# Moving a sample's past scores to just behind a job's values, in the differential-attention rounds of a decoder step

## The reference, cut to what matters

```
p = probs(q1, k1) - lam * probs(q2, k2)     # softmax each, over all keys
o = einsum('bhts,bshd->bthd', p, v)
# prompt: keys = its own 512 tokens, causal
# sample: keys = 1024 past keys from the pages, then its 8 new ones
```

## Time and profile before

| what | value |
|---|---|
| median of 3 runs | 2305.47 us (2305.38 to 2305.98) |
| the profiled execution, its own time | 2303.8 us |
| its span, first to last instruction | 2302.0 us |
| mean granted clock of TensorE | 0.979 of full |
| differential rounds (first past scores to last values) | 127.0 to 274.3 us of the span |
| first past scores to the last sample's past scores, 7 rounds | 127.0 to 257.6 us, 18.7 us a round |

### The profile page before, as it was taken

How to read it: one execution, slowest core, us unless ns; L and a number is a source line. 1 busy time by engine, 2 the same in 40 slices (tenths; PEclk the granted TensorE clock), 3 DMA queues, 4 the chain that set the end, 5 groups by cost and what they waited for, 6 DMA issues and landing times.

```text
span 2302.0 us, 37427 instructions
## 1 busy us (share of the span) xinstructions
PE 2121.5 (92%) x15226; PEld 1875.4 (81%) x15230; DVE 1233.9 (54%) x2035; ACT 708.7 (31%) x1085; POOL 269.8 (12%) x243
## 2 busy tenths in 40 slices
PE   8978899989998999999999899888998999999997
PEld 6745688778877999999997577567987999999996
DVE  4346456755543566426544799564433466524642
ACT  5233344432231322212233425342322322212222
POOL 0012101530100100000002235320100100000001
PEclk9999999989999999999999999999999999999998
DMA  5366423323343222222224124642343222222221
GB/s 184 112 213 221 156 65 105 125 78 129 119 176 115 81 74 83 74 83 78 74 80 119 49 81 160 202 129 73 122 155 133 82 74 78 79 83 74 83 70 58
DMA packets 220861, 249.28 MB, mean 108 GB/s; under 512 B 18498, under 2 KB 175436, under 8 KB 220486
## 3 DMA queue, kind: packets, MB, share of 16 engines
q1 hardware_dynamic: 199162, 196.22, 26.9%
q0 software_dynamic: 9936, 28.78, 3.9%
q10 hardware_dynamic: 11592, 21.88, 2.8%
HBM read 233.63 MB, written 13.00 MB: 107 GB/s over the span
## 4 chain that ended last, share of the span: by engine, by line
PE 76%; DVE 12%; issue 5%; ACT 3%; DMA 2%; PEld 2%; POOL 1%; PEldq 0%; DVEq 0%; POOLq 0%; SPq 0%; ACTq 0%
PE PS L831 52%; PE PS L810 5%; PE PS L888 5%; PE PS L1244 1%; DVE arena L3189 1%; PE PS L1259 1%; DVE arena L3187 1%; DVE arena L3222 1%; DVE arena L3219 1%; DVE stat L2516 1%; PE PS L1431 1%; DVE arena L2423 1%; PE PS L1560 1%; PE PS L964 1%; PEld PS L1097 1%
## 5 line engine op out<-in xcount | busy, mean ns | idle before, releaser
L831 PE MATMUL PS<-hT_r,WH 128*128 128x288 f32 (+2 forms) x1856 | 554.0, 298 | 21.7 <-issue 17.1
L831 PE MATMUL PS<-xr_r,WH 128*128 128x288 f32 (+2 forms) x1920 | 571.6, 298 | 1.6 <-POOL W_r L658 1.6
L831 PE MATMUL PS<-hT_r,W_r 128*128 128x288 f32 (+2 forms) x1856 | 549.7, 296 | 0.0
L2380 DVE TENSOR_TENSOR W_r<-W,WH 128x1024 fp32r<-128x1024 f32 (+1 forms) x219 | 284.0, 1317 | 375.1 <-ACT WH L1695 374.3
L831 PE MATMUL PS<-arena_r,WH 128*128 128x224 f32 (+2 forms) x1920 | 441.5, 298 | 3.7 <-issue 3.7
L1695 ACT ACTIVATE WH<-W 128x1024 fp32r<-128x1024 f32 (+1 forms) x262 | 266.1, 1034 | 501.3 <-PE PS L831 275.8
L831 PEld LDWEIGHTS PS<-hT_r,WH 128*128 128x128 f32 x1856 | 350.2, 189 | 35.0 <-issue 31.6
L831 PEld LDWEIGHTS PS<-xr_r,WH 128*128 128x128 f32 x1920 | 364.0, 190 | 2.3 <-issue 2.3
L831 PEld LDWEIGHTS PS<-hT_r,W_r 128*128 128x128 f32 x1856 | 350.3, 189 | 0.0
L831 PEld LDWEIGHTS PS<-arena_r,WH 128*128 128x128 f32 x1920 | 326.9, 190 | 6.4 <-issue 6.3
L831 PE MATMUL PS<-arena_r,W_r 128*128 128x288 f32 (+2 forms) x704 | 208.6, 296 | 0.0
(11 more groups left out here) (439 smaller groups left out, 3054.6 us busy)
## 6 DMA issues: line engine op xcount, KB each, us to landing
W<-in_w_ffn_in SPq DMA_DIRECT2D x176, 256.0 KB, 3.3
W<-in_w_ffn_out SPq DMA_DIRECT2D x40, 512.0 KB, 3.4
W<-in_w_in_ab SPq DMA_DIRECT2D x28, 512.0 KB, 3.7
C<-in_cache_mem_k SPq DMA_DIRECT2D x10, 1024.0 KB, 7.8
C<-in_cache_diff_k POOLq DMA_DIRECT2D x32, 256.0 KB, 4.0
C<-in_cache_diff_k SPq DMA_DIRECT2D x32, 256.0 KB, 3.3
C<-in_cache_diff_v POOLq DMA_DIRECT2D x32, 256.0 KB, 5.1
C<-in_cache_diff_v SPq DMA_DIRECT2D x32, 256.0 KB, 4.9
```

The costliest lines, as they stand in the source:

```text
L831: ins = mm(o, w[:, k, c * 128:c * 128 + 128], v(k0 + k)[:, t0:t1], start=opens and first and k == 0 and e == 0, stop=last and k == nk - 1 ...
L2380: v_.tensor_tensor(slot_view(WL, NW, n), slot_view(W, NW, n), plain(slot_view(WH, NV, n)), ALU.subtract).then_inc(lo_done, 1)
```

## The change

PE: the past scores and the new scores of a sample are two functions now. The past scores of sample b+1 are issued right behind `prompt_values(2b)`, between steps 6 and 7, one half of the keys after the other; each half waits only for the copies of its own transposes, and the first for the exponentials of sample b. The mask and the new scores stay where they were, behind `sample_turn(b)`, and carry the signal to DVE; they no longer wait for all copies. The first sample's scores, ahead of the rounds, are as they were.

DVE: of the two key copies that followed `prompt_max(2b)`, the one of head 0 stands ahead of it now. ACT, SP, POOL and every instruction's shape are unchanged.

```
-            def sample_scores(b):
-                wait_tr()
+            def past_scores(b, turned):
                 if b:
                     pe.wait_ge(handoff["s_exp"], b)
-                as_scores(b, sreg(0)).then_inc(handoff["s_scores"], 1)
+                for c in range(2):
+                    wait_tr(turned[c])
+                    as_past_scores(b, sreg(0), c)
+
+            def new_scores(b):
+                as_new_scores(b, sreg(0)).then_inc(handoff["s_scores"], 1)
...
                 prompt_values(2 * b, one)
+                if b + 1 < NB:
+                    past_scores(b + 1, keys)
                 two = prompt_probs(2 * b + 1)
                 sample_turn(b)
                 if b + 1 < NB:
-                    sample_scores(b + 1)
+                    new_scores(b + 1)
...
             for b in range(NB):
+                if b + 1 < NB:
+                    as_keys("DADA", 0, range(1))
                 prompt_max(2 * b)
                 if b + 1 < NB:
-                    as_keys("DADA", 0)
+                    as_keys("DADA", 0, range(1, H))
                 sample_normal(b)
```

More of the change, by code:

```diff
@@ L959, in ap_values, with as_past_scores, as_new_scores @@
                 return ins
[L961 to L965, removed]
+            def as_past_scores(b, s, c):
+                for h in range(H):
+                    mm(s[32 * h:32 * h + 32, 512 * c:512 * c + 512], qz[:, b, h, :], KT[:, h, 512 * c:512 * c + 512],
+                       start=True, stop=True)
+            def as_new_scores(b, s):
                 if b:
@@ L1042, in _ @@
             tj.use(5, 6, 7)
-            sample_scores(0)
+            past_scores(0, [len(tj.who)] * 2)
+            new_scores(0)
             for b in range(NB):
+                keys = []
                 prompt_scores(2 * b)
@@ L1047, in _ @@
                     as_keys("DADA")
+                    keys.append(len(tj.who))
                 if b > 0:
@@ L2559, in _, with as_keys @@
             lr, ms_ = L["lrow"], const("mapsel")
-            def as_keys(whos, half):
-                for h in range(H):
+            def as_keys(whos, half, heads=range(H)):
+                for h in heads:
                     tr_copy(whos[h], L["KT_a"][:, h, half * 512:half * 512 + 512])
```

## The result

The changed kernel took 2285.41 us (median of 4 runs, 2283.17 to 2288.35) against 2305.43 us: a ratio (changed over before, so below 1 is faster) of 0.9917 with a 95% interval of 0.9894 to 0.9940. It is faster, by 20.0 us between the medians, where 16.0 was forecast and the range began at 2286.5. The profiled execution took 2288.35 us with a span of 2286.6, only 15.4 us shorter than the span before. That these two differences don't agree is the first thing to explain.

A forecast was written before the change was run, and what follows sets the result against it. PE was taken to bound the stage behind the rounds, with PE's waits in the seven rounds to be saved. 14.3 + 2.4 + 0.3 - 1.0 = 16.0 us off 2305.47 gave 2289.5 us, range 2286.5 to 2296.0.

The forecast's parts named there:

- The handover: From job 2b's values to the next sample's mask, PE's waits vanish in all seven rounds: 14.3 us gained.
- the two slow handovers: Into rounds 1 and 3 the past scores ran at half clock; full clock expected, gains of 3.11 and 3.23 us.
- The key copy: Head 0's earlier copy lets the nine transposes start sooner in rounds 1 to 6: 2.4 us gained.
- The loads: Shorter rounds use up DMA pauses, delaying the second half of the keys: 1.0 us lost, bounds 0 to 3.5.
- The conversion to the whole: Whole kernel: subtract 16.0 us from a median 1.67 us above the profiled execution; measurement tells apart about 4.6 us.
- Rival 1: Handover clock falls remain, or loads cost their upper bound, with the copy worthless: gain 9 to 13.5 us; chance 0.20.
- Rival 2: Clock falls once per round between new scores and sample's values: 2297.9 us; chance 0.05 with other gains of 4.6 to 9.
- Rivals 3 and 4: Slow clock from new scores to sample's values each round, 2318 us, chance 0.03; new place still waits, 2305 us, 0.05.
- rival 5: Loads cost nothing and round 7's clock fall goes too: gain 18.5 to 20 us, about 2286.5; chance 0.05.

The follow-up runs named there:

- filler: Kernel before, plus four matmuls of the next sample's past scores right behind `prompt_values(2b)`, overwritten later by the real ones; ratios 1.0026 and, repeated, 1.0031.
- before, again: The kernel before, unedited, run and traced a second time; ratio 1.0008, rounds 147.7 us.
- Copy only: Kernel before with only DVE's part of the change, head 0's key copy ahead of the job's maximum; ratio 0.9982, rounds 144.0 us.
- scores twice: Changed kernel with the past scores of samples 1 to 7 computed again at their old place ahead of the mask; median 2302.0 us, ratio 0.9988.

## Why the prediction was right and where it was wrong

**The handover: right.** Forecast 14.3 us, measured 34.83 - 20.27 = 14.6 (means of the traces). The parts held to 0.03 us, the clock stayed up at the handovers in all traces with the past scores moved, and the filler speaks for the work there as the reason. A little luck is in the sum: the forecast took the two slow handovers from one trace, and the second trace of before has two as well, but one of them in another round.

**The key copy: right in size, incomplete in cause.** Forecast 2.4, measured 31.6 - 29.4 = 2.2 us. I bounded the effect of the late job maximum on ACT by 0 and 0.64 us and took 0; in round 5 it was 0.24. That cost nothing in the changed kernel, since DVE's `sample_normal` ends the wait as late, and only moving `sample_normal` away made it visible. Rounds 5 and 6 gave 0.14 us each where I had 0.22.

**The loads: wrong, and this is the term that failed.** The step was "A tail of the loads before could delay this one by 0 to 0.5 us a round; I take 1.0 us", with 0.3 us gained in round 0: 0.7 us lost. In its place the stretch from the nine transposes to the values of job 2b, in which the wait for the load lies, went from a mean of 58.3 to 56.6 us: 1.7 gained. PE's waits for in_cache_diff_k in it were 1.6 and 2.6 us before and 0.2, 2.0 and 0.8 after, 2.1 and 1.0 in the mean; part of the rest is the slow clock that before, again has there. I had seen that DMA pauses would be used up, and that release and want move together; but from a smaller pause does not follow a wait, and half the values' bytes changed nothing. Copy only has the lowest sum, 55.3, which fits an earlier release of the place; but a single trace, with waits that change by 1 to 2 us between executions of one kernel, does not prove it. So it is shown that the loads cost the changed kernel nothing steady; that the change made their waits shorter is not shown.

**The rest:** the head of round 0 and the last round lost 0.8 us together in the mean. 14.6 + 2.2 + 1.7 - 0.8 = 17.7 us is what the rounds gained, 147.7 to 130.0, against 16.0. These 1.7 us more would not alone have left the range: 2305.47 - 17.7 is 2287.8.

**The conversion to the whole: wrong in its certainty.** "The median of the runs lies 1.67 above it" and "about 0.2%, 4.6 us" treat a kernel's time as one number. The three runs shown lay within 0.6 us; many runs spread over 18. The first four of the changed kernel gave 20.0, all of them 18.3, which is the rounds' 17.7 within the error. The other 2.3 us of the miss are therefore outside the rounds, in that first draw of four, and the forecast had no term for it. A range built from the cases of the change alone missed by 1.1 us; with the spread of a median of four runs (the single runs have a standard deviation of 3.5 to 4.1 us, so an estimate of some 2 to 3 us either way) it would have held 2285.4.

**The rivals.** Rival 1 was wrong in all its mechanisms: the clock did not fall at the handovers, the loads cost nothing steady, and the copy was worth 2.2 us. Rival 2, the clock falling in each round elsewhere, did not happen: in the changed kernel's three traces the clock is full from round 1 until after the mask of round 7, and so the sentence of the Trainium skill (TensorE: Matmul & The Clock Gate, section on PE-mode transpose), that a transpose doesn't count as busy in the same way, gave the wrong forecast where transposes and short matmuls alternate. Rivals 3 and 4 did not occur; of rival 5, loads that cost nothing was the true half, and the slow clock of round 7 stayed in all three traces of the changed kernel, so that its number came close by luck.

**Open.** Why the filler kernel is slower behind the rounds, where its instructions are those of the kernel before. The size is accounted for, by the time at 1.2 GHz (95.6 and 92.2 us against 64.9 and 80.4), and both traces have it; what sets the number of falls there is not found. Nor is it shown whether the change itself moves that number.

## What to carry to other kernels

Look for work whose inputs have long been ready and put it into the wait before it, in front of what still has to be awaited; if the trace then has no bracket between the two, the gain is the sum of the waits and of the small joints beside them (in round 1 here 1.95 us, where the two brackets name 1.71), and start-to-start distances forecast it to a few hundredths. Where a wait has one name, the engine that comes second may be late by as much. And compare the stretch that was edited between repeated traces before believing a difference of the whole that is smaller than the spread of many runs.

## What the runs showed of the hardware

Executions of one kernel, each on one core, spread by 0.8% over three chips (2296.9 to 2314.8 us) and by 0.7% on one of them (2296.9 to 2312.5), much more than the first three suggested, and the time follows the mean granted clock. The same 13,400 matmuls behind the rounds took 2014 to 2032 us, with the time spent at 1.2 GHz, 59 to 96 us, but not strictly: 59.8 us of it went with 2017.5 and 59.2 with 2014.2. Windows over that part in the traces of scores twice and filler, columns as in the earlier trace rows:

```profile
267.48:2281.00 2013.52, 1892.64 (x13424) 1714.22 (x13428) 1092.49 (x1694) 601.60 (x874) 234.53 (x175) 0.99 0.31 98
```

```profile
271.29:2303.00 2031.71, 1908.78 (x13426) 1726.99 (x13430) 1092.63 (x1694) 601.46 (x874) 235.77 (x175) 0.98 0.30 97
```

DVE, ACT and the bytes are the same, PE's busy time is 16 us longer. The eight f32 matmuls of the past scores, four of them side by side in the array, took 1.92 us at the full clock, and 3.64 us in the first sample's past scores of the changed kernel, where the granted clock was 0.50 from 124 to 129 us.
